# Modulation pieces behind the mixers, inside the router's logits and behind the sums that follow each expert stage

## What is computed

```python
def adaln(cvec, w_mod, b_mod):
    m = jax.nn.silu(cvec) @ w_mod + b_mod            # (1024) @ (1024, 6 * 1024)
    return [t[:, None, :] for t in jnp.split(m, 6, axis=-1)]

for i in range(DEPTH):
    sc1, ac1, gc1, sc2, ac2, gc2 = adaln(c_ctx[None, :], w_mod[i], b_mod[i])
    sl1, al1, gl1, sl2, al2, gl2 = adaln(c, w_mod[i], b_mod[i])
    hc = rmsnorm(xc, norm1_g[i]) * (1 + ac1) + sc1
    ...                                              # mixer i
    xc = xc + gc1 * yc
    hc2 = rmsnorm(xc, norm2_g[i]) * (1 + ac2) + sc2
    xc = xc + gc2 * moe(hc2, router_w, router_b, moe_wg[i], moe_wu[i], moe_wd[i])
```

## Time and profile before

| | us |
|---|---|
| three runs, median (lowest to highest) | 1785.13 (1782.42 to 1789.11) |
| the profiled execution | 1786.43 |
| its span, first to last instruction | 1784.6 |
| PE busy in it | 1697.7 (95%) |
| DVE, ACT, POOL busy | 466.6, 368.7, 37.9 |
| loaded and stored by DMA | 612.11 MB, mean 343 GB/s |
| mean granted TensorE clock | 0.979 of full speed |

### The profile page before, as it was taken

The page is one execution under the profiler, slowest core; times in us unless marked ns, Lnnn a source line. Parts: engine busy times, 40 slices in busy tenths (PEclk is TensorE's granted clock), DMA queues, the critical chain, the costliest instruction groups (busy, mean ns, idle before and its releaser), DMA issues.

```text
span 1784.6 us, 21218 instructions
## 1 busy us (share of the span) xinstructions
PE 1697.7 (95%) x8603; PEld 979.9 (55%) x8603; DVE 466.6 (26%) x1245; ACT 368.7 (21%) x749; POOL 37.9 (2%) x49
## 2 busy tenths in 40 slices
PE   5999999999999999999998999999999999999996
PEld 3577544436744887734434657844443787444443
DVE  2142511105304220411112154431111353410112
ACT  2132300003133620400002124310000342100001
POOL 1000000000000000000000000000000000000000
PEclk9999999999999999899999999999999999999998
DMA  9989699999997249499999697689999738799993
GB/s 357 382 287 385 273 428 428 427 427 342 372 336 281 97 167 384 162 424 428 428 429 397 254 357 282 250 335 427 428 428 418 276 113 360 296 428 428 428 428 143
DMA packets 134763, 612.11 MB, mean 343 GB/s; under 512 B 12485, under 2 KB 19285, under 8 KB 109576
## 3 DMA queue, kind: packets, MB, share of 16 engines
q1 hardware_dynamic: 117408, 589.84, 82.4%
q10 hardware_dynamic: 12824, 12.85, 2.2%
q0 software_dynamic: 4432, 8.02, 1.2%
HBM read 608.81 MB, written 8.94 MB: 346 GB/s over the span
## 4 chain that ended last, share of the span: by engine, by line
PE 82%; DMA 11%; DVE 3%; ACT 2%; issue 1%; SPq 1%; ACTq 0%; DVEq 0%
PE PS L1580 22%; PE PS L1007 21%; PE PS L1591 11%; PE PS L1544 7%; DMA ring<-in_moe_wg 6%; PE PS L1037 4%; PE PS L1093 3%; DVE arena L2144 2%; DMA out_C<-small 2%; DMA ring<-in_attn_w_qkv 1%; PE PS L1524 1%; PE PS L1061 1%; DMA ring<-in_w_mod 1%; PE PS L1585 1%; PE PS L1529 1%
## 5 line engine op out<-in xcount | busy, mean ns | idle before, releaser
L1580 PE MATMUL PS<-ring,arena 128*64 128x512 f32 x1280 | 367.6, 594 | 7.6 <-DMA ring<-in_moe_wg 7.6
L941 ACT ACTIVATE arena<-PS 128x512 f32<-128x512 f32 (+1 forms) x130 | 70.7, 544 | 804.9 <-PE PS L1571 343.7
L1580 PEld LDWEIGHTS PS<-ring,arena 128*64 128x64 f32 x1280 | 115.6, 137 | 185.1 <-issue 183.9
L1007 PE MATMUL PS<-HS,ring 128*128 128x256 f32 x896 | 199.4, 380 | 0.0
L2144 DVE TENSOR_TENSOR arena<-arena,PS 128x512 f32<-128x512 f32 x32 | 33.5, 1048 | 613.2 <-PE PS L1580 613.2
L1007 PEld LDWEIGHTS PS<-HS,ring 128*128 128x128 f32 x896 | 168.9, 190 | 27.4 <-issue 5.1
L1580 PE MATMUL PS<-arena 128*64 128x512 f32 x576 | 169.7, 594 | 0.4 <-DMA arena<-in_moe_wg 0.4
L1544 PE MATMUL PS<-arena 128*128 128x256 f32 (+3 forms) x688 | 144.6, 361 | 5.9 <-ACT arena L941 3.7
L1591 PE MATMUL PS<-ring,arena 128*64 128x512 f32 x640 | 146.0, 607 | 2.5 <-DVE arena L2125 2.5
L1544 PEld LDWEIGHTS PS<-arena 128*128 128x128 f32 (+1 forms) x688 | 112.2, 190 | 44.9 <-issue 22.7
L1007 PE MATMUL PS<-arena,ring 128*128 128x256 f32 x512 | 114.5, 384 | 2.1 <-ACT arena L690 1.1
(11 more groups left out here) (338 smaller groups left out, 1523.5 us busy)
## 6 DMA issues: line engine op xcount, KB each, us to landing
ring<-in_w_mod SPq DMA_DIRECT2D x48, 2048.0 KB, 16.7
ring<-in_moe_wu SPq DMA_DIRECT2D x41, 2048.0 KB, 22.1
ring<-in_moe_wd SPq DMA_DIRECT2D x41, 2048.0 KB, 23.1
ring<-in_moe_wg SPq DMA_DIRECT2D x41, 2048.0 KB, 21.5
arena<-in_moe_wg SPq DMA_DIRECT2D x24, 2048.0 KB, 20.8
HS<-in_moe_wu SPq DMA_DIRECT2D x12, 2048.0 KB
arena<-in_moe_wu SPq DMA_DIRECT2D x12, 2048.0 KB, 22.1
arena<-in_moe_wd SPq DMA_DIRECT2D x12, 2048.0 KB, 26.7
```

The lines of the kernel that those rows point to most:

```text
L941: A(dst, src, func).then_inc(S(sem), 1)
L1007: ins = mm(out, a, b, start=first and i == 0, stop=final and i == len(pairs) - 1)
L1580: ins = mm(PS[64 * e:64 * e + 64, b, :], XG[:, k, 64 * e:64 * e + 64], w[:, k], start=(k == 0), stop=(k == KD - 1))
```

## The change

It regroups the 48 pieces in nine groups and moves 13 of them:

- three pieces go behind each of the mixers 0, 1 and 2: one behind the sum of squares, where four fillers were; one in two halves inside the logits, behind the third and the sixth tile; one ahead of the gather, where one filler was. Behind mixer 3 stands one piece, in place of four fillers.
- one piece goes behind the sum of squares that follows each of the expert stages 0, 1 and 2, in place of four fillers.
- three fillers behind the `ht` transposes become one in the layers 0 to 2.

The first attention keeps 9 of 12 pieces, the mLSTM 11 of 16, the gated linear attention 8 of 12, the last attention 3 of 4. Groups behind a mixer gather in PSUM bank 6, so the first gather goes to banks 0 and 1 instead of 6 and 7; ACT copies them ahead of pair 0's weights, PE turns them (`mod_cols`) behind pair 0's first `up`, DVE adds the bias ahead of pair 0. The three chunks of such a group stand in SP's list ahead of the layer's expert chunks, so they take three of the ring's six slots there; `early()` moves from q7, q5, q7 to q6, q5, q6 in the layers 0, 1 and 2, and q2 goes ahead of q8 instead of behind it.

```diff
-MODS = [ORDER[a:b] for a, b in ((0, 4), (4, 16), (16, 32), (32, 44), (44, 48))]
-GMODS = (0, 2, 4, 6, 8, 10, 12)
+MODS = [ORDER[a:b] for a, b in ((0, 4), (4, 13), (13, 16), (16, 28), (28, 31), (31, 40), (40, 43), (43, 47), (47, 48))]
+GMODS = (1, 2, 4, 5, 6, 8, 9)
+MMODS = (1, 2, 4, 6, 8, 9, 10, 11, 12, 12, 12, 12, 12)
...
-            chunks += [("qkv", 3, c) for c in (2, 0, 1)] + mod(3, 8, 12) + [("wo", 3, c) for c in range(2)]
+            chunks += mod(7, 0, 1) + [("qkv", 3, c) for c in (2, 0, 1)] + mod(7, 1) + [("wo", 3, c) for c in range(2)]
+        chunks += mod(behind_mixer(l))
         chunks += [(w, l, p + NPAIR * e) for p in range(NPAIR) for w in ("wg", "wu", "wd") for e in range(2)]
...
                 for q in range(SPARE, SPARE + RING):
-                    if q == (7, 5, 7, 3)[l]:
+                    if q == (6, 5, 6, 3)[l]:
                         early()
+                    if q == SPARE + RING - 1:
+                        sp.wait_ge(S("ht"), 4 * (l + 1))
+                        load(n + SPARE - 1)
                     load(n + q)
-                sp.wait_ge(S("ht"), 4 * (l + 1))
-                load(n + SPARE - 1)
...
                 n = len(MODS[g])
-                mod_run(l + 1, n - 4, n - 3)
+                if l == 0:
+                    mod_run(g, n - 4, n - 3)
                 turn_probs(6)
...
                         ins = mm(bank(4 + s, 0, NE), H[:, k, T * s:T * s + T], RW[:, k], start=(k == 0), stop=(k == KD - 1))
+                    if k in (2, 5):
+                        mod_rows(gb, 1, range(4) if k == 2 else range(4, KD))
                 ins.then_inc(S("logit"), 1)
...
-                warm(WARM[2])
+                warm(1 if len(MODS[gb]) > 2 else WARM[2], 7)
...
-                warm(WARM[3])
+                mod_rows(gb, 2)
                 pe.wait_ge(S("pw"), 36 * l + 4)
-                gather(BANKS[1], "gather")
+                gather((0, 1), "gather")
...
                     sumsq(2 * l)
-                    warm(WARM[0])
+                    mod_rows(in_mixer(l), 0)
                 (lambda: attention(l // 3, l), mlstm, gla)[l % 3]()
                 sumsq(2 * l + 1)
-                warm(WARM[1])
+                mod_rows(behind_mixer(l), 0)
```

More of the change, by code:

```diff
@@ L106, with in_mixer, behind_mixer, mod_group @@
 ORDER = [(l, c) for l in range(DEPTH) for c in range(12)]
-MODS = [ORDER[a:b] for a, b in ((0, 4), (4, 16), (16, 32), (32, 44), (44, 48))]
-GMODS = (0, 2, 4, 6, 8, 10, 12)
+MODS = [ORDER[a:b] for a, b in ((0, 4), (4, 13), (13, 16), (16, 28), (28, 31), (31, 40), (40, 43), (43, 47), (47, 48))]
+def in_mixer(l):
+    return 2 * l + 1
+def behind_mixer(l):
+    return 2 * l + 2
+def mod_group(l, c):
+    return next(g for g, group in enumerate(MODS) if (l, c) in group)
+GMODS = (1, 2, 4, 5, 6, 8, 9)
+MMODS = (1, 2, 4, 6, 8, 9, 10, 11, 12, 12, 12, 12, 12)
 def mod_parts(g):
@@ L133, in plan_chunks @@
     chunks = []
-    mod = lambda l, lo, hi: [("mod", l, c) for c in range(lo, hi)]
-    chunks += mod(0, 0, 4)
-    chunks += [("qkv", 0, 2)] + mod(0, 4, 8) + [("qkv", 0, 0)] + mod(0, 8, 12) + [("qkv", 0, 1)] + mod(1, 0, 4)
+    mod = lambda g, lo=0, hi=12: [("mod", *u) for u in MODS[g][lo:hi]]
+    chunks += mod(0)
+    chunks += [("qkv", 0, 2)] + mod(1, 0, 4) + [("qkv", 0, 0)] + mod(1, 4, 5) + [("qkv", 0, 1)] + mod(1, 5, 9)
     chunks += [("wo", 0, 0), ("wo", 0, 1)]
@@ L323, in program @@
         YSS, YR = sm(0, 2, 2), sm(8, 2)
-        MP = [ar(8000, 512), ar(8000, 512), ar(8192, 512), sq(1536, 512), ar(8000, 512)]
+        RSF = RS[:, :, :].rearrange("p a b -> p (a b)")
+        MP = [ar(8000, 512), ar(8000, 512), RSF, ar(8192, 512), RSF, sq(1536, 512), RSF, ar(8000, 512), RSF]
+        MB = [7 if g % 2 or g == 0 else 6 for g in range(len(MODS))]
         QT = ar(0, 8, N2)
@@ L627, in mods @@
                 act.wait_ge(S("mod_rows"), ORDER.index(MODS[g][-1]) + 1)
-                run(A(MP[g], bank(7), ACT.Copy), "mod_sb")
+                run(A(MP[g], bank(MB[g]), ACT.Copy), "mod_sb")
             eps1 = c_("eps")[0:1]
@@ L775, in mlstm @@
                     if i == 7:
-                        mods(2)
+                        mods(in_mixer(1))
                     if i < 2:
@@ L1029, in _, with mod_rows @@
             after(pe, "cs")
-            def mod_rows(g, i):
+            def mod_rows(g, i, ks=range(KD)):
+                if i >= len(MODS[g]):
+                    return
                 l, c = MODS[g][i]
                 w = landed(pe, POS["mod", l, c])
-                for k in range(KD):
+                for k in ks:
                     r = 32 * (k % 4)
-                    ins = mm(PS[r:r + 32, 7, :], CS[:, k, 30 - 2 * i:62 - 2 * i], w[:, k], start=(i == 0 and k < 4), stop=(i == len(MODS[g]) - 1 and k >= 4))
-                ins.then_inc(S("mod_rows"), 1)
+                    ins = mm(PS[r:r + 32, MB[g], :], CS[:, k, 30 - 2 * i:62 - 2 * i], w[:, k], start=(i == 0 and k < 4), stop=(i == len(MODS[g]) - 1 and k >= 4))
+                if k == KD - 1:
+                    ins.then_inc(S("mod_rows"), 1)
             def mod_run(g, lo, hi):
@@ L1277, in mlstm @@
                         scores(1)
-                mod_cols(2)
+                mod_cols(in_mixer(1))
                 def turn(u):
@@ L1493, in gla @@
                 output(1)
-                mod_cols(3)
+                mod_cols(in_mixer(2))
                 output(2)
@@ L1614, in pair @@
                             slot_id()
+                            mod_cols(gb)
                         if not first and g == 0:
@@ L1831, in attention @@
                 turned_probs(7)
-                mods(l + 1)
+                mods(in_mixer(l))
                 divide(7)
@@ L2183, in moe @@
                 go(v.tensor_copy(IDX[:, 1:NPAIR], idf), "idx")
+                mods(behind_mixer(l))
                 pair(n0, 0)
```

58 lines of the change are left out of this document (32 added, 26 removed).

## The result

The changed kernel takes **1792.81 us** (median of 11 runs, the lowest 1787.64) against 1783.18 for the kernel before, run beside it on the same chip: a ratio of **1.0053, 95% interval [1.0039, 1.0066]**, 9.5 us slower. The forecast was 1779.9, with a range up to 1791: both the sign and the range were wrong.

What follows compares the result with a forecast made beforehand. PE bounds the mixers; PE and the full weight stream, within some 2 us, end the expert stages. Layers 0 to 3: +3.0 - 9.1 + 1.6 - 0.7 = -5.2 us, giving 1779.9 us; range 1762 to 1791 (8 in 10).

Steps and rivals of the forecast that it cites:

- Pieces leaving the mixers: Mixers: PE sheds 13 pieces of 1.8 us; 5.3, 8.9, 6.3 and 0.7 us won in layers 0 to 3.
- The last state store: End of layer 1's mLSTM: head 7's store, right behind q4, q0 and q1, takes 15 us, between 3.6 and 24.3.
- +3.4: Ahead of layer 1's sum: PE, held by ACT's squares behind the last store, is done at 715.5 instead of 712.1.
- Rival 2: Layer 1: state stores queue one after the other behind the burst, layer 1 gains nothing (+1); 1790 us, chance 0.15.
- Behind the sum: Sum to gather: pieces in and behind the logits against fewer fillers, together -0.5 us, ends +3 and -2, counting in layer 1.
- rival 3: Layer 1: clock stays down to the gather, piece +1.8, gather some +2, gain 5.3 instead of 9.1; 1784 us, chance 0.12.
- The weight stream: Expert stages of layers 0 and 2: more chunks left than the earlier start makes up, +3.0 and +1.6 us.
- Rival 1: Layers 0 and 2: the stream doesn't bind and they keep PE's gain, -21.4 us in all; 1764 us, chance 0.22.
- Rival 4: Layers 0 and 2: weights slower among stores and gathered rows, 5.9 us a chunk, +7 us each; 1794 us, chance 0.04.
- rival 5: Moved pieces: their chunks aren't there when PE comes; one miss, 4.9 us, makes it 1785 us; chance 0.02.
- Layer 3: Last layer: nothing changes but the 0.7 us of one moved piece, -0.7 us, between -1.8 and 0.
- layer 1's miss: Layer 1 was forecast at -9.1 us (-8.9 - 5.2 + 3.4 + 2.1 - 0.5), ends -13 and +1.

Runs made afterwards that it cites:

- run 1: Changed kernel with layer 1's expert chunks q0 and q1 issued behind q6 instead of q4: 1783.96 us, ratio 1.0008 to the kernel before.
- run 2: Changed kernel with ACT's two waits for `out_C` moved behind its wait for the sum of squares: 1784.05 us, ratio 1.0012 to the kernel before.
- run 3: Changed kernel with the piece inside the logits put whole ahead of them: 1785.85 us, ratio 1.0028 to the kernel before.
- run 10: Changed kernel with q0 and q1 issued behind q4 in layers 0 and 2, behind q5 in layer 1: 1772.38 us, ratio 0.9936.
- run 6: Changed kernel with q0 and q1 of layers 0 and 2 issued behind q4 instead of q5: 1783.86 us, ratio 1.0009 to the kernel before.
- run 9: Kernel before, with q0 and q1 issued behind q4 in layers 0 and 2, behind q5 in layer 1: 1786.27 us, ratio 1.0011.
- run 4: Changed kernel with the filler ahead of layer 3's gather put back: 1791.99 us, ratio 1.0055 to the kernel before.
- run 12: Changed kernel with only the last of the eight products of the logits' piece made, leaving work out: 1759.42 us, a total that can't be used.

## Why the prediction was wrong, step by step

- **Pieces leaving the mixers: right.** 5.3, 6.3 and 0.7 us were forecast in the layers 0, 2 and 3; the sums there start 7.0, 6.2 and 0.7 us earlier in their layers, 1.7 of the first being a stretch of full clock. In layer 1 PE comes to the sum 15.9 us earlier in its layer (1.7 of it again clock), forecast were 14.1, with the pause for the state's stores gone.
- **The last state store: right mechanism, wrong size.** "Its price lies between 3.6 and 24.3 us; I take 15, since the burst is that long." It took 22.3. The term "+3.4" became 10.4 us of waiting. Run 1 takes this wait away and run 2 half of it, and each is 7 to 8 us faster. Between ends that far apart I took the burst's length, though the only row with a store beside a burst had 24.3. Rival 2 priced layer 1 at the measured +1, but by another road: head 5's store had landed by 692.7, as the burst was issued, and only the last two heads were caught.
- **Behind the sum: the step that failed.** "Together -0.5 us, with +3 and -2 as ends." Measured: +3.6, +6.2, +6.0 and +1.9, and in the other profiles still some +2 and more in the layers 0 and 2. I had costed the halves of the piece at what ACT's pace leaves free, and the piece ahead of the gather at 1.8 us, both at full clock. But the clock falls inside the logits in both kernels, before too (0.79 to 0.84 in the stretch), and there ACT's pace hid it. A piece put in front of the fall pushes more logits behind it, and its second half lies behind it itself. From the first logit to the ranks it takes 12.6 and 14.1 us in the layers 0 and 2, before 10.2 and 10.8. Run 3's profile is 2.5 to 5.4 us shorter, part of that by where the clock fell in this execution.

  The other part of the miss stands ahead of the gather: in the runs 1 and 10 the logits of the layers 0 and 2 run at full clock and take 6.1 to 6.2 us, no more than the 6.5 of the forecast, but the piece behind the ranks runs at half clock there, 3.5 to 3.6 us, and from the ranks to the gather it takes 4.9 to 5.0 us instead of 2.3: +2.7, where I had +0.5. This is near rival 3, which I had at 0.12 and priced at this piece and the gather, in layer 1 alone. In the changed kernel the clock was down until 745.1 in layer 1, when the gather begins (3.77 us, full), and through the piece ahead of it (3.56 us instead of 1.8): the piece is as this rival has it, the gather is not. By the Trainium skill, "TensorE: Matmul & The Clock Gate", Part 4: PE-mode transpose, a transpose doesn't count as PE-busy in the same way; in layer 2 of run 3 they run at full clock and the fall comes 3 us behind them, in the changed kernel it comes ahead of them, so no run here decides it.
- **The weight stream: right.** +3.0 and +1.6 stand against +1.7 and +3.1, wg of the last pair was forecast at 385 and came at 384.4, and runs 3, 6, 9 and 10 show each side of it. Rival 1 fell. The wait at the second `up` of pair 0 came in layer 0 (2.4 us, not 3 to 6) and not in layer 2, since PE itself was late. Rival 4 fell too: 428 GB/s again. So did rival 5: PE waits for no chunk of `w_mod` in the changed kernel. (The pair whose start is read at 300.88 and 327.55 in the prediction begins there with its first `up`, on `wg`, and not its second; the 26.7 us are right.)
- **Layer 3: a term left out.** I costed the order of SP and one piece, but not the filler that vanishes: +1.9 (run 4). Another 1.7 us is in the last pair: its first `up`, behind a wait of 2.3 us for `wg`, met a fall of the clock (at 1724.7) and took 8.8 us instead of 7.1. Of the other profiles only run 1's has a layer 3 as long from first to last `up` (207.2 us against 205.1 to 205.7), so this part isn't tied to the change.

In sum: of layer 1's miss of 9.9 us, 5.2 lie ahead of the sum (the store 7.0 too dear, less 1.7 of clock won) and 4.6 behind it; layer 3 adds 3.6, the layers 0 and 2 together nearly nothing, since the stream covers there both what PE wins and what it loses. Both large mistakes are of one kind: a middle price (15 us, full clock) for a moment of which the rows of before showed the dear one.

## What to carry to other kernels

- Work moved out of a stage that the engine bounds is won only if the stream that bounds the next stage starts earlier by as much. Look for its last idle moment, and put transfers that have a free place in front of it: that was worth 21 us here, and nothing in the kernel before.
- A store on which an engine waits must not share the queue's engines with a burst of loads. Issue the burst behind it, if need be by a wait on the store.
- Work put between short products cost more here than the same work ahead of them (run 3), and a filler that goes without a successor is to be counted as a change.
- A stretch in which the clock falls differs by 4 us between profiles that have the same products in it (22.8 to 26.9 us in layer 2). What an edit does to it is read from several profiles, not from one.

## What the runs showed that I had not expected

- The stores of the last two heads, 128 KB each, took 7 to 10 us to land behind one chunk of 2 MB (run 1) and 14 to 22.3 us behind three, though chunks and stores have queues of their own. The stretch 696 to 704 of the changed kernel (queue, packets, MB, share of 16 engines; weights are q1, stores q10):

```profile
q1 hardware_dynamic: 214, 3.24, 95.0%
q10 hardware_dynamic: 212, 0.11, 4.5%
```

  The two queues move packet for packet in this stretch, and a packet of the weights is some 30 times as large. The Trainium skill, "DMA: Bandwidth & Descriptors", Queues, rings and completion order, says that a DMA engine serves its queues in turn, packet by packet; the equal counts of packets agree.
- PE stands still for 4.0 us once in an execution, beside one packet (16 KB) of the instruction queue, while weights fill the queues. Its place moved by a whole layer with the change, and that shifts an account by layers by 6 us; in run 12 it came nowhere. Such a packet lies beside the sums without a gap too: there it starts 1.5 to 2.0 us behind the sum's start (at 970.70 behind 969.07 in the changed kernel), and where the gap is, 2.7 to 2.8 us ahead of it (1386.56 ahead of 1389.31). That fits a load of code that comes too late, but it wasn't tried, nor was the branch on surplus experts that stands in PE's stream ahead of each of these sums. The Trainium skill, "Runtime: NRT & Kernel Launch", Instruction fetch mechanics, calls crossing such a block mostly hidden; if the packet is the cause, it wasn't hidden here.
- The same sixteen transposes take 1.94 us or 3.65 us, by where the clock's fall lies. In layer 2 the fall comes 5.6 us behind the sum in the changed kernel's profile and 15.3 us behind it in run 1's, whose edit concerns layer 1 alone.
